# FFN down projections with one 512-column matmul per activation block for its high and low part

## The chip, the cores and the metric

The kernel runs on one core of one Trainium2 chip. The metric is device time in microseconds (us) of one launch. Durations of single instructions are in nanoseconds (ns).

## The reference

Two stacked transformer blocks of two layers each, on 256 tokens (T) of width 1024. There are eight SwiGLU feed-forward parts (FFNs); all else (attention of several kinds, retention, gated linear attention, cross attention, projections) is not touched by the change. An FFN is

```python
def swiglu(h, w_in, w_out):
    g, u = split_cols(h @ w_in, (D_FF, D_FF))      # D_FF = 2816
    return (jax.nn.silu(g) * u) @ w_out            # the last product is the "down projection"
x = x + 0.5 * swiglu(rms_norm(x, g), w_in, w_out)
```

Inputs and outputs are float32.

## The kernel before

Everything is kept transposed: a block is 128 channels (partitions) by 256 tokens. The 1024 channels are 8 blocks (KB), the 2816 hidden channels 22 blocks (HB). A product in nearly full precision is made of three matmuls in the float32r format: every weight tile `w` is split into `w_hi` (ScalarE, line 998) and `w_lo = w - w_hi` (VectorE, line 1410), every activation block into a high and a low part, and TensorE sums `w_hi*a_hi + w_hi*a_lo + w_lo*a_hi` in a PSUM bank.

The work of TensorE is a list of **units**. A unit is up to eight 128x128 weight tiles (k blocks) for one block of outputs, so 24 matmuls of 256 columns (18 where there are only six k blocks). Weights come from memory in loads of 1 MB (eight k blocks by 256 output channels, so two units) into a ring of four buffers, issued on SyncE's queue; the split weights lie in rings of four units. A splitting waits until the unit that used the slot four units earlier is done.

A **down projection** (`down0` to `down7`) has 8 output blocks. The 22 k blocks of an output are three units (8, 8 and 6 blocks); the two outputs of a 256-channel column chunk take turns, so their last units (two with 6 k blocks) come one after the other. That is 24 units and 528 matmuls for each down projection: 176 times `w_hi*hid_hi` (line 610), 176 times `w_hi*hid_lo` (line 611), and 176 times `w_lo*hid_hi` (line 614). Within a unit lines 610 and 611 alternate over the k blocks, and then line 614 runs over them. TensorE loads a weight tile before every matmul, also before the second that uses the same tile. The accumulator `acc` has four banks of 512 float32; a unit uses the first 256 columns of one (`out_ap`, line 491). Activations are in `hid_hi` and `hid_lo`, two tensors of 22 blocks.

The order of all work is written out by hand in one function `order`, which each engine goes through with its own stages. For a down projection the stage is `residual`. When an output block is complete, VectorE evicts it: line 1525 reads PSUM, scales it by 0.5 and by `rstd` (the norm's factor for each token) into `hidf`, waits for its own result (`link`), and line 1527 adds that to the residual stream `x`. Then it makes `w_lo` of a coming unit (`split_after`), and then the low part of the new `x` block for the next stage (`low`, line 1464), which waits for ScalarE's high part (line 1036). ScalarE squares the block (line 1040), and GpSimd adds the squares up (line 1924).

The next stage begins with a **leading pair** of units (`lead_pair`, lines 579 to 581): six matmuls for each block j, each j waiting for both parts of block j of the new `x`. Behind the pair TensorE takes the sum of the squares (line 649), for which it waits for GpSimd's last addition; where the next stage holds no values it then runs three small transposes of `x` (line 657) whose result nobody reads, and else two-column matmuls (line 652).

Of the kernel before, what the change touches and what calls it, by code (L numbers as in the profile page):

```python
# [9 lines left out]
F32R = mybir.dt.float32r  # L10
I32 = mybir.dt.int32
ALU = mybir.AluOpType
ACT = mybir.ActivationFunctionType
AX = mybir.AxisListType

P = 128
T = 256
# [3 lines left out]
HB = FF // P  # L21
# [7 lines left out]
BANKS = 4  # L29
# [153 lines left out]
def build(nc, io, out):  # L183
    loads, units, outs, lin = plan_stream(io)
# [3 lines left out]
    for _, kind in outs:  # L188
        count[kind] += 1
        freed.append((kind, count[kind]))  # L190
# [15 lines left out]
    with ExitStack() as ctx:  # L206
        def sb(name, shape, dt=F32):
            return ctx.enter_context(nc.sbuf_tensor(name, shape, dt))

        def sem(name):  # L210
            return ctx.enter_context(nc.semaphore(name))
# [9 lines left out]
        w_hi = sb("w_hi", [P, RING, 8, P], F32R)  # L221
        w_lo = sb("w_lo", [P, RING, 8, P], F32R)
# [9 lines left out]
        silu_g, hidf = gates_hid[:, 0:2, :], gates_hid[:, 2:4, :]  # L232
        small = sb("small", [P, 64])
        rstd = sb("rstd", [P, 2, T])
        wa2 = sb("wa2", [P, 512])
        pos = sb("pos", [P, T], I32)
        with nc.sbuf_tensor("hid_hi", [P, HB, T], F32R) as hid_hi, nc.sbuf_tensor("hid_lo", [P, HB, T], F32R) as hid_lo:
            pass

        work = sb("work", [P, 2 * HB, T])  # L240
        ident, ones, ones64, perm_rope, perm_ret = (mats[:, i, :] for i in range(5))
# [3 lines left out]
        acc = ctx.enter_context(nc.psum_tensor("acc", [P, BANKS, 512], F32))  # L245
# [5 lines left out]
        w_hi_ready, w_lo_ready, unit_done = sem("w_hi_ready"), sem("w_lo_ready"), sem("unit_done")  # L251
# [3 lines left out]
        silu_done, hid_mul, hid_hi_ready, hid_lo_ready = sem("silu_done"), sem("hid_mul"), sem("hid_hi_ready"), sem("hid_lo_ready")  # L255
# [235 lines left out]
        def out_ap(o):  # L491

            return acc[:, o % BANKS, 0:T]

        def wait_free(eng, o):

            if o >= BANKS:
                kind, n = freed[o - BANKS]
                eng.wait_ge((gate_evac, hid_mul, out_evac)[kind], n)
# [38 lines left out]
        fills = {"hn": (hn_hi, hn_lo, hn_hi_ready, hn_lo_ready), "mn": (mn_hi, mn_lo, mn_hi_ready, mn_lo_ready)}  # L538
# [25 lines left out]
        def _(pe):  # L564
            s = Stages()
            state = Progress()

            def lead_pair(i):
# [15 lines left out]
                if state.sums is not None:  # L584
                    sum_squares()

            def unit(i):
                u = units[i]
                if i in leaders:
                    return lead_pair(i)  # L590
                if i - 1 in leaders:
                    return
                if u.first:
                    wait_free(pe, u.out)
                pe.wait_ge(w_hi_ready, i + 1)
                if u.src == "hid":
                    a_hi, a_lo = hid_hi, hid_lo
                    pe.wait_ge(hid_hi_ready, u.need)
                    pe.wait_ge(hid_lo_ready, u.need)
                else:  # L600
                    a_hi, a_lo, r_hi, r_lo = fills[u.src]
                fresh = u.src != "hid" and (i == 0 or units[i - 1][8:10] + (units[i - 1].k0,) != u[8:10] + (u.k0,))
                if u.mode == "F":
                    wh, wl = w_hi[:, u.slot], w_lo[:, u.slot]
                    bank = out_ap(u.out)
                    for j in range(u.nk):
                        if fresh:
                            pe.wait_ge(r_hi, 8 * u.need + u.k0 + j + 1)
                            pe.wait_ge(r_lo, 8 * u.need + u.k0 + j + 1)
                        nc.tensor.matmul(bank, wh[:, j, :], a_hi[:, u.k0 + j, :], start=u.first and j == 0, stop=False)  # L610
                        nc.tensor.matmul(bank, wh[:, j, :], a_lo[:, u.k0 + j, :], start=False, stop=False)  # L611
                    pe.wait_ge(w_lo_ready, i + 1)
                    for j in range(u.nk):
                        mm = nc.tensor.matmul(bank, wl[:, j, :], a_hi[:, u.k0 + j, :], start=False,  # L614
                                              stop=u.last and j == u.nk - 1)
                else:

                    if fresh:
                        pe.wait_ge(r_hi, 8 * u.need + 8)
                        pe.wait_ge(r_lo, 8 * u.need + 8)  # L620
                    pair, t = u.slot - u.half, u.half
                    pe.wait_ge(w_hi_ready, i - u.half + 2)
                    pe.wait_ge(w_lo_ready, i - u.half + 2)
                    bank = out_ap(u.out).rearrange("p (s n) -> p s n", s=2)
                    for j in range(u.nk):
                        ah, al = a_hi[:, j, P * t:P * t + P], a_lo[:, j, P * t:P * t + P]
                        wh, wl = w_hi[:, pair:pair + 2, j, :], w_lo[:, pair:pair + 2, j, :]
                        nc.tensor.matmul(bank, ah, wh, start=j == 0, stop=False)  # L628
                        nc.tensor.matmul(bank, ah, wl, start=False, stop=False)  # L629
                        mm = nc.tensor.matmul(bank, al, wh, start=False, stop=j == u.nk - 1)  # L630
                mm.then_inc(unit_done, 1)

                if state.sums is not None and u.src == "hn" and i >= BANKS - 1:
                    sum_squares()
# [9 lines left out]
            def sum_squares():  # L644

                i, column = state.sums
                state.sums = None
                pe.wait_ge(squares_added, 7 * (i + 1))
                mm = nc.tensor.matmul(wide[:, 0, 0:T], ones, t1[:, 0, :], start=True, stop=True)
                if column:  # L650
                    for t in range(2):
                        mm = nc.tensor.matmul(wide[:, 1, 2 * t:2 * t + 2], t1[:, 0, P * t:P * t + P], ones[:, 0:2],
                                              start=True, stop=True)
                mm.then_inc(sums_done, 1)
                if not column:
                    for b in range(3):
                        nc.tensor.transpose(wide[:, 1, P * b:P * b + P], x[:, b, 0:P], ident)
# [735 lines left out]
        def _(dve):  # L1393
            s = Stages()
            state = Progress()

            def link(ins):

                state.chain += 1
                ins.then_inc(dve_chain, 1)  # L1400
                dve.wait_ge(dve_chain, state.chain)

            def split_after(i):

                while state.split < len(units) and (units[state.split].free or 0) <= i + 1:
                    n, u = state.split, units[state.split]
                    dve.wait_ge(w_hi_ready, n + 1)
                    if u.free is not None:
                        dve.wait_ge(unit_done, u.free)
                    nc.vector.tensor_tensor(w_lo[:, u.slot, 0:u.nk, :], raw[:, u.raw % RING, 0:u.nk, P * u.half:P * u.half + P],  # L1410
                                            w_hi[:, u.slot, 0:u.nk, :].bitcast(F32), ALU.subtract).then_inc(w_lo_ready, 1)
                    state.split = n + 1
# [102 lines left out]
            def residual(c, name, scale, gain):  # L1515
                l, later = lin[name], []
                if name in PARTED:
                    dve.wait_ge(out_evac, freed[l.o0 - 1][1])
                for n in range(l.u0, l.u1):
                    u = units[n]  # L1520
                    if u.last:
                        k = u.out - l.o0
                        dve.wait_ge(unit_done, n + 1)
                        if u.src == "hid":
                            link(nc.vector.scalar_tensor_tensor(hidf[:, k % 2, :], out_ap(u.out), scale, rstd[:, 0, :],
                                                                ALU.mult, ALU.mult))
                            nc.vector.tensor_tensor(x[:, k, :], x[:, k, :], hidf[:, k % 2, :], ALU.add).then_inc(out_evac, 1)
                        else:
                            nc.vector.tensor_tensor(x[:, k, :], x[:, k, :], out_ap(u.out), ALU.add).then_inc(out_evac, 1)
                        if gain is not None:  # L1530
                            later.append(k)
                    if n < l.u1 - (2 if name in PARTED else 1):
                        split_after(n)
                    for k in later:
                        low(k, c.gen, gain)
                    later = []
                split_after(l.u1 - 1)
                dve.wait_ge(out_evac, freed[l.o1 - 1][1])
# [543 lines left out]
```

## Time and profile before

| what | us |
|---|---|
| three runs shown | 2218.0, 2218.53, 2229.66; median 2218.53 |
| span of the profiled execution, first to last instruction | 2228.6 |
| its own time, taken to be the run of 2229.66 (the only one that is not shorter than the span) | 2229.66 |
| mean granted clock of TensorE in it | 0.994 of 2.4 GHz |
| TensorE busy with matmuls / weight loads | 2167.5 / 2123.3 |
| VectorE / ScalarE / GpSimd busy | 1508.9 / 1182.3 / 117.6 |

Matmuls overlap in the records, since the end of one is modelled with its way through the array. So what tells how fast TensorE works is the distance from one start to the next, or the number of matmuls in a stretch, and not a matmul's duration. Records are named by line, engine and operation, then output<-inputs (moving operand first, then the weights), shapes, and in brackets the idle time of the engine before it with what ended that.

### The profile page before, as it was taken

To read this page: it belongs to the slowest core of one execution; us is meant where nothing else is said; L and a number is where in the kernel's file an instruction comes from. 1 tells how busy PE (TensorE), PEld (TensorE's weight loads), DVE (VectorE), ACT (ScalarE), POOL (GpSimd) and SP (SyncE) were. 2 spreads that over 40 slices of the span, in tenths; PEclk is the share of its full clock that TensorE was granted. 3 is DMA by queue.
4 is the path that set the end of the run, shared out by engine and by line. 5 is a ranking of instruction groups with operands and counts; after the bars stand their busy time and mean duration, and the time that the engine had idled before them with its cause. 6 is when DMAs were issued, how large, how long until landed. Compare 5 with 4: busy or idle time off the path is not lost.

```text
span 2228.6 us, 44915 instructions
## 1 busy us (share of the span) xinstructions
PE 2167.5 (97%) x18339; PEld 2123.3 (95%) x18339; DVE 1508.9 (68%) x2244; ACT 1182.3 (53%) x1852; POOL 117.6 (5%) x140
## 2 busy tenths in 40 slices
PE   5999999999999999999999999999999999999998
PEld 5999987899999999989999999989999999999998
DVE  5756668676667666686766666688666666667664
ACT  5644455565456444465654554546655554556543
POOL 2101000110011000000100000100000000001001
PEclk9999999999999999999999999999999999999999
DMA  7556443365565656542765665644656665636653
GB/s 240 182 180 190 140 145 95 105 218 190 186 192 177 197 186 215 167 143 76 229 197 180 199 193 191 231 138 137 205 185 194 198 200 179 191 105 191 197 180 105
DMA packets 383402, 392.76 MB, mean 176 GB/s; under 512 B 6800, under 2 KB 381712, under 8 KB 383072
## 3 DMA queue, kind: packets, MB, share of 16 engines
q1 hardware_dynamic: 381632, 383.30, 53.8%
q0 software_dynamic: 1568, 6.59, 0.8%
q8 instruction: 148, 2.42, 0.5%
q14 instruction: 54, 0.44, 0.1%
HBM read 388.81 MB, written 1.05 MB: 175 GB/s over the span
## 4 chain that ended last, share of the span: by engine, by line
PE 86%; DVE 6%; ACT 4%; issue 2%; POOL 1%; DMA 1%; SPq 0%; POOLq 0%; ACTq 0%; DVEq 0%
PE acc L610 24%; PE acc L611 24%; PE acc L614 24%; DVE w_lo L1410 2%; PE acc L628 2%; PE acc L630 2%; PE acc L629 2%; ACT w_hi L998 2%; PE acc L579 1%; PE acc L581 1%; PE acc L580 1%; POOL t L1924 1%; DMA raw<-in_ffn_w_in 1%; PE wide L804 1%; PE wide L702 0%
## 5 line engine op out<-in xcount | busy, mean ns | idle before, releaser
L1410 DVE TENSOR_TENSOR w_lo<-raw,w_hi 128x1024 fp32r<-128x1024 f32 (+2 forms) x790 | 898.7, 1141 | 489.7 <-ACT w_hi L998 487.5
L998 ACT ACTIVATE w_hi<-raw 128x1024 fp32r<-128x1024 f32 (+2 forms) x790 | 775.6, 988 | 832.7 <-PE acc L614 755.2
L610 PE MATMUL acc<-hn_hi,w_hi 128*128 128x256 f32 x3328 | 791.9, 280 | 24.9 <-DMA colc<-in_cols 17.8
L611 PE MATMUL acc<-hn_lo,w_hi 128*128 128x256 f32 x3328 | 786.4, 278 | 0.0
L610 PEld LDWEIGHTS acc<-hn_hi,w_hi 128*128 128x128 f32 x3328 | 629.2, 189 | 29.0 <-DMA colc<-in_cols 17.8
L611 PEld LDWEIGHTS acc<-hn_lo,w_hi 128*128 128x128 f32 x3328 | 629.3, 189 | 0.6 <-issue 0.5
L614 PE MATMUL acc<-hn_hi,w_lo 128*128 128x256 f32 x3328 | 449.7, 278 | 0.0
L614 PEld LDWEIGHTS acc<-hn_hi,w_lo 128*128 128x128 f32 x3328 | 412.9, 189 | 0.0
L610 PE MATMUL acc<-hid_hi,w_hi 128*128 128x256 f32 x1408 | 331.6, 277 | 0.0
L611 PE MATMUL acc<-hid_lo,w_hi 128*128 128x256 f32 x1408 | 331.6, 277 | 0.0
L611 PEld LDWEIGHTS acc<-hid_lo,w_hi 128*128 128x128 f32 x1408 | 264.8, 188 | 0.0
L610 PEld LDWEIGHTS acc<-hid_hi,w_hi 128*128 128x128 f32 x1408 | 264.8, 188 | 0.0
L1924 POOL TENSOR_TENSOR t<-t 128x256 f32<-128x256 f32 x119 | 107.2, 901 | 2102.0 <-ACT t L1040 2054.7
L614 PE MATMUL acc<-hid_hi,w_lo 128*128 128x256 f32 x1408 | 192.4, 277 | 0.0
L614 PEld LDWEIGHTS acc<-hid_hi,w_lo 128*128 128x128 f32 x1408 | 175.2, 188 | 0.0
L610 PE MATMUL acc<-mn_hi,w_hi 128*128 128x256 f32 x512 | 131.6, 293 | 4.5 <-DVE mn_lo L1512 3.7
L611 PE MATMUL acc<-mn_lo,w_hi 128*128 128x256 f32 x512 | 125.8, 282 | 0.0
L610 PEld LDWEIGHTS acc<-mn_hi,w_hi 128*128 128x128 f32 x512 | 98.1, 192 | 7.0 <-issue 6.7
L1545 DVE TENSOR_TENSOR gates_hid<-acc,rstd 128x256 f32<-128x256 f32 x176 | 74.4, 423 | 37.8 <-PE acc L614 26.8
L611 PEld LDWEIGHTS acc<-mn_lo,w_hi 128*128 128x128 f32 x512 | 98.0, 191 | 1.4 <-issue 1.2
L1554 DVE TENSOR_TENSOR gates_hid<-gates_hid,acc 128x256 f32<-128x256 f32 x176 | 73.9, 420 | 28.6 <-PE acc L614 26.9
L1464 DVE SCALAR_TENSOR_TENSOR hn_lo<-x,gains,hn_hi 128x256 fp32r<-128x256 f32 x112 | 79.2, 712 | 12.3 <-ACT hn_hi L1036 12.3
(250 smaller groups left out, 2178.1 us busy)
## 6 DMA issues: line engine op xcount, KB each, us to landing
raw<-in_ffn_w_in SPq DMA_DIRECT2D x88, 1024.0 KB, 5.2
raw<-in_ffn_w_out SPq DMA_DIRECT2D x32, 1024.0 KB, 5.3
raw<-in_ffn_pre_w_gate SPq DMA_DIRECT2D x22, 1024.0 KB, 5.4
raw<-in_ffn_pre_w_up SPq DMA_DIRECT2D x22, 1024.0 KB, 5.4
raw<-in_ffn_post_w_gate SPq DMA_DIRECT2D x22, 1024.0 KB, 5.3
raw<-in_ffn_post_w_up SPq DMA_DIRECT2D x22, 1024.0 KB, 5.4
raw<-in_x_w_kv SPq DMA_DIRECT2D x16, 1024.0 KB, 5.5
raw<-in_ffn_pre_w_down SPq DMA_DIRECT2D x16, 1024.0 KB, 5.1
```

What stands on the lines that cost most here:

```text
L610: nc.tensor.matmul(bank, wh[:, j, :], a_hi[:, u.k0 + j, :], start=u.first and j == 0, stop=False)
L611: nc.tensor.matmul(bank, wh[:, j, :], a_lo[:, u.k0 + j, :], start=False, stop=False)
L614: mm = nc.tensor.matmul(bank, wl[:, j, :], a_hi[:, u.k0 + j, :], start=False, stop=u.last and j == u.nk - 1)
L628: nc.tensor.matmul(bank, ah, wh, start=j == 0, stop=False)
L629: nc.tensor.matmul(bank, ah, wl, start=False, stop=False)
L630: mm = nc.tensor.matmul(bank, al, wh, start=False, stop=j == u.nk - 1)
L998: nc.scalar.activation(w_hi[:, u.slot, 0:u.nk, :], raw[:, u.raw % RING, 0:u.nk, P * u.half:P * u.half + P], ACT.Copy).then_inc(w_hi_ready, 1)
L1410: nc.vector.tensor_tensor(w_lo[:, u.slot, 0:u.nk, :], raw[:, u.raw % RING, 0:u.nk, P * u.half:P * u.half + P], w_hi[:, u.slot, 0:u.nk, :]. ...
L1464: nc.vector.scalar_tensor_tensor(hn_lo[:, k, :], x[:, k, :], gains[:, gain + k:gain + k + 1], hn_hi[:, k, :].bitcast(F32), ALU.mult, ALU.s ...
L1545: nc.vector.tensor_tensor(silu_g[:, h, :], out_ap(units[u0 + h].out), rstd[:, 0, :], ALU.mult)\
L1554: nc.vector.tensor_tensor(hidf[:, h, :], silu_g[:, h, :], out_ap(units[u0 + 2 + h].out), ALU.mult).then_inc(hid_mul, 1)
L1924: nc.gpsimd.tensor_tensor(t1[:, 0, :], t1[:, 0, :], t1[:, k, :], ALU.add).then_inc(squares_added, 1)
```

## The change

High and low part of a hidden block lie side by side in one tensor, and one matmul with 512 columns takes both into the two halves of the bank. The part with `w_lo` is added to the first half as before. The eviction first adds the two halves with a `tensor_reduce` over a strided view of the bank, and the scaling then reads its result from SBUF instead of PSUM.

```diff
-        with nc.sbuf_tensor("hid_hi", [P, HB, T], F32R) as hid_hi, nc.sbuf_tensor("hid_lo", [P, HB, T], F32R) as hid_lo:
-            pass
+        with nc.sbuf_tensor("hid", [P, HB, 2, T], F32R) as hid:
+            hid_hi, hid_lo = hid[:, :, 0, :], hid[:, :, 1, :]
...
+        def both_out(o):
+
+            return acc[:, o % BANKS, 0:2 * T]
...
+            def hidden_unit(i):
+
+                u = units[i]
+                if u.first:
+                    wait_free(pe, u.out)
+                pe.wait_ge(w_hi_ready, i + 1)
+                pe.wait_ge(hid_hi_ready, u.need)
+                pe.wait_ge(hid_lo_ready, u.need)
+                for j in range(u.nk):
+                    nc.tensor.matmul(both_out(u.out), w_hi[:, u.slot, j, :], hid[:, u.k0 + j, :, :].rearrange("p s t -> p (s t)"),
+                                     start=u.first and j == 0, stop=False)
+                pe.wait_ge(w_lo_ready, i + 1)
+                for j in range(u.nk):
+                    mm = nc.tensor.matmul(out_ap(u.out), w_lo[:, u.slot, j, :], hid[:, u.k0 + j, 0, :], start=False,
+                                          stop=u.last and j == u.nk - 1)
+                mm.then_inc(unit_done, 1)
...
                         if u.src == "hid":
-                            link(nc.vector.scalar_tensor_tensor(hidf[:, k % 2, :], out_ap(u.out), scale, rstd[:, 0, :],
+                            link(nc.vector.tensor_reduce(hidf[:, k % 2, :], both_out(u.out).rearrange("p (s t) -> p t s", s=2),
+                                                         AX.X, ALU.add))
+                            link(nc.vector.scalar_tensor_tensor(hidf[:, k % 2, :], hidf[:, k % 2, :], scale, rstd[:, 0, :],
                                                                 ALU.mult, ALU.mult))
                             nc.vector.tensor_tensor(x[:, k, :], x[:, k, :], hidf[:, k % 2, :], ALU.add).then_inc(out_evac, 1)
```

`unit` calls `hidden_unit` for the units of the down projections; their waits are the same as before. All other units are unchanged.

## Rows read from the trace of the kernel before

**Rows 1.** The page's first part: busy us, share, instructions.

```profile
PE 2167.5 (97%) x18339; PEld 2123.3 (95%) x18339; DVE 1508.9 (68%) x2244; ACT 1182.3 (53%) x1852; POOL 117.6 (5%) x140
```

**Rows 2.** The page's costliest groups: matmuls of the down projections; last, idle before.

```profile
L610 PE MATMUL acc<-hid_hi,w_hi 128*128 128x256 f32 x1408 | 331.6, 277 | 0.0
L611 PE MATMUL acc<-hid_lo,w_hi 128*128 128x256 f32 x1408 | 331.6, 277 | 0.0
...
L614 PE MATMUL acc<-hid_hi,w_lo 128*128 128x256 f32 x1408 | 192.4, 277 | 0.0
```

**Rows 3.** Stretches: us, busy (count) of PE, PEld, DVE, ACT, POOL; PEclk, DMA share, GB/s.

```profile
154.00:216.00 62.00, 62.00 (x529) 62.00 (x528) 37.18 (x46) 29.61 (x39) 4.38 (x5) 1.00 0.60 189
597.00:656.00 59.00, 59.00 (x523) 59.00 (x523) 36.53 (x47) 28.82 (x38) 4.25 (x5) 1.00 0.60 192
783.00:844.00 61.00, 61.00 (x520) 61.00 (x520) 36.25 (x46) 28.68 (x38) 4.41 (x5) 1.00 0.57 182
```

**Rows 4.** Timeline of PE, start and us: line 614 of successive units, down0 and down1.

```profile
155.75 1.10 PE L614 MATMUL acc<-hid_hi,w_lo 128*128 128x256 f32 x8
158.57 1.10 PE L614 MATMUL acc<-hid_hi,w_lo 128*128 128x256 f32 x8
...
601.36 1.07 PE L614 MATMUL acc<-hid_hi,w_lo 128*128 128x256 f32 x8
604.08 1.07 PE L614 MATMUL acc<-hid_hi,w_lo 128*128 128x256 f32 x8
```

**Rows 5.** Timeline of PE's weight loads before matmuls 256, 2 and 512 wide.

```profile
427.80 1.27 PEld L773 LDWEIGHTS wide<-work 128*128 128x128 f32 x6
429.10 1.08 PEld L783 LDWEIGHTS wide<-mats,t 128*128 128x128 f32 x8
430.09 0.19 PEld L610 LDWEIGHTS acc<-hn_hi,w_hi 128*128 128x128 f32 x1
...
924.81 0.19 PEld L686 LDWEIGHTS wide<-t,mats 128*128 128x128 f32 x1 [0.24 <-issue]
...
926.96 0.19 PEld L686 LDWEIGHTS wide<-t,mats 128*128 128x128 f32 x1 [0.24 <-issue]
```

**Rows 6.** Busy time by stretch, columns as in rows 3: up parts, and behind down2.

```profile
100.00:150.00 50.00, 50.00 (x427) 50.00 (x426) 31.81 (x45) 24.59 (x36) 0.00 (x0) 1.00 0.59 191
...
664.00:688.00 24.00, 24.00 (x214) 24.00 (x213) 17.74 (x25) 17.38 (x30) 5.75 (x6) 1.00 0.64 211
...
720.00:770.00 50.00, 50.00 (x427) 50.00 (x426) 34.46 (x50) 26.50 (x40) 0.00 (x0) 1.00 0.66 212
860.00:910.00 50.00, 50.00 (x427) 50.00 (x426) 38.39 (x59) 18.90 (x18) 0.00 (x0) 1.00 0.62 197
...
1280.00:1330.00 50.00, 50.00 (x443) 50.00 (x443) 33.71 (x48) 24.77 (x37) 0.00 (x0) 1.00 0.61 190
```

**Rows 7.** Groups of DVE by line and shape: busy us, mean ns.

```profile
L1527 DVE TENSOR_TENSOR x<-x,gates_hid 128x256 f32<-128x256 f32 x64 | 27.4, 428 | 2.2
L1525 DVE SCALAR_TENSOR_TENSOR gates_hid<-acc,rstd 128x256 f32<-128x256 f32 x64 | 26.6, 415 | 6.7 <-PE acc L614 6.7
...
L1626 DVE TENSOR_REDUCE small<-prob 128x2 f32<-128x512 f32 x16 | 10.8, 676 | 0.0
...
L1582 DVE SCALAR_TENSOR_TENSOR t<-keep,gains,t 128x256 f32<-128x256 f32 x16 | 7.5, 479 | 4.5 <-ACT t L1028 4.5
```

**Rows 8.** Timeline of DVE, then POOL and PE, where down1 ends at 656.6.

```profile
655.54 0.43 DVE L1527 TENSOR_TENSOR x<-x,gates_hid 128x256 f32<-128x256 f32 x1
655.99 1.23 DVE L1410 TENSOR_TENSOR w_lo<-raw,w_hi 128x1024 fp32r<-128x1024 f32 x1
657.13 0.97 DVE L1464 SCALAR_TENSOR_TENSOR hn_lo<-x,gains,hn_hi 128x256 fp32r<-128x256 f32 x1
658.02 0.41 DVE L1525 SCALAR_TENSOR_TENSOR gates_hid<-acc,rstd 128x256 f32<-128x256 f32 x1
...
659.46 0.48 DVE L1464 SCALAR_TENSOR_TENSOR hn_lo<-x,gains,hn_hi 128x256 fp32r<-128x256 f32 x1 [0.58 <-ACT hn_hi L1036]
...
659.82 0.73 POOL L1924 TENSOR_TENSOR t<-t 128x256 f32<-128x256 f32 x1 [2.00 <-ACT t L1040]
...
661.43 0.28 PE L579 MATMUL acc<-hn_hi,w_hi 128*128 128x256 f32 x1
...
662.11 0.59 PE L649 MATMUL wide<-t,mats 128*128 128x256 f32 x2
```

**Rows 9.** Timeline at the end of down7, the last projection of the kernel.

```profile
2218.83 0.42 DVE L1525 SCALAR_TENSOR_TENSOR gates_hid<-acc,rstd 128x256 f32<-128x256 f32 x1 [1.16 <-PE acc L614]
...
2221.01 0.70 PE L649 MATMUL wide<-t,mats 128*128 128x256 f32 x2 [2.22 <-POOL t L1924]
```

More of the change, by code:

```diff
@@ L592, in unit @@
                     return
+                if u.src == "hid":
+                    return hidden_unit(i)
                 if u.first:
@@ L595, in unit @@
                 pe.wait_ge(w_hi_ready, i + 1)
[L596 to L602, printed above, removed]
+                a_hi, a_lo, r_hi, r_lo = fills[u.src]
+                fresh = i == 0 or units[i - 1][8:10] + (units[i - 1].k0,) != u[8:10] + (u.k0,)
                 if u.mode == "F":
```

## The prediction

> **What bounds the kernel now.** I read the page's busy shares first: TensorE's matmuls cover 97% of the span, its weight loads 95%, VectorE 68% [rows 1]. Then the groups of the down projections: 3 x 1408 matmuls, and no idle time of TensorE before any of them [rows 2]. So the down projections are bound by TensorE, and what one matmul costs there is the distance between two starts. The busy time by stretch gives it by count: down1 runs 523 matmuls in 59.0 us, 112.8 ns each, and down0 529 in 62.0 us, 117.2 ns [rows 3]. The timeline gives it exactly: a unit of 24 matmuls takes 604.08 - 601.36 = 2.72 us in down1, 113.3 ns for each, and 158.57 - 155.75 = 2.82 us in down0, 117.6 ns [rows 4]. So there are **two paces**, at the same granted clock (1.00, which is 2.4 GHz) in both [rows 3]. Down0 and down2 went at the slow pace, the other six at the fast one (their stretches count 523 matmuls in 59 us, as down1). The pace holds for long stretches and is not bound to the code: the up part of the third FFN began fast behind down1 (214 in 24 us), then turned slow and stayed so through down2 and behind it (427 in 50 us); the first FFN was slow too, the up part of the fifth fast (443) [rows 6]. That is much of what separates the runs: the 11 us between this execution's own time (2229.66, its span of 2228.6 and about 1.1 around it) and the median of 2218.53 are 2500 slow matmuls at 4.4 ns, more than either slow stretch holds (some 200 us, 1700 to 1850 matmuls). So the median run had at most one of the two slow down projections.
>
> **The merged pair, the main term.** 1408 pairs of 256-column matmuls with the same weights become 1408 matmuls of 512 columns. A pair costs 2 x 113.3 = 226.7 ns, or 235.2 at the slow pace. What will 512 columns cost? That depends on what the 113.3 are: the streaming of the columns, or the weight load before each. The load's own pace shows where matmuls have only 2 columns: from the first to the last of the group starting at 429.10, to 430.09, is 0.99 us for 8 loads, of which the first distance is still that of the 256-wide one before it (the group at 427.80 has (429.10 - 427.80)/6 = 217 ns each); the other seven take (990 - 217)/7 = 110 ns [rows 5]. So a weight load alone takes 110 ns, nearly the whole 113.3. The streaming: plain float32 matmuls with 512 columns start (926.96 - 924.81)/5 = 430 ns apart, those with 256 columns 217 [rows 5], so 256 more columns cost 213 and the fixed part is about 3 ns. Float32 takes over 1.9 times as long for a column as float32r (430/512 against 113.3/256), so I take it to stream everything twice: 512 float32r columns then stream as 256 float32 ones, in **216 ns**, with the load of the next tile hidden under them (the load takes 110 of the 216 there too). The bounds: below, 213 (the columns alone); above, 226.7 (nothing gained). I take 216, the row with as much streaming and one load. Saved: 10.8 ns a pair at the fast pace, 19.3 at the slow one; 1408 x 10.8 = 15.2 us, and for each slow down projection another 176 x 8.5 = 1.5.
>
> The Trainium skill, "TensorE: Matmul & The Clock Gate", section "Back-to-back issue gap", gives N/2.4 + 2.5 ns for a lone matmul: 109.2 ns for 256 columns and 215.8 for 512. The trace agrees for the wide float32 ones and not for the 256-wide float32r ones, which take 113.3. By that rule a merger would save one fixed part, 2.5 ns, and the whole change 3.5 us before its costs; it is the second rival below.
>
> **The remaining narrow matmuls.** The 1408 with `w_lo` keep 256 columns, in runs of 8 or 6 behind 512-wide ones. Which pace a run takes is drawn anew after each break in the stream, and no row shows it behind 512-wide float32r matmuls. All fast costs nothing; all slow costs 1408 x 4.4 = 6.2 us against a fast execution. With no reason for either I take the middle, 3.1 us (and half of it, 0.4 us, back for each down projection that was slow).
>
> **The eviction, 64 times.** It gains a reduction over 512 elements: 676 ns by the reduction with 512 inputs [rows 7]. Bounds: below, 0.42 (a 256-wide instruction), above 1.23, the row with 1024 elements [rows 8], if each short sum of two costs double. Line 1525 goes from reading PSUM (415 ns) to two operands in SBUF, 479 as line 1582 [rows 7], and the extra link costs about 0.04. Together 0.78 us. In the middle of a down projection this is hidden: VectorE is busy 36.5 of 59 us [rows 3], and 8 x 0.78 = 6.2 us more still leaves 16 us idle; `w_lo` is made for a unit that runs three units, some 8 us, later. Memory has room too (0.60 busy in these stretches). The changed layout of `hid` changes no instruction's size.
>
> **Where the cover is thin: the end of a down projection, 7 times.** VectorE is late there already. Last matmul of down1 at 656.6; its eviction starts only at 658.02, behind the eviction of block 6, a `w_lo` and a `hn_lo`; `hn_lo` of block 7 ends at 659.94, and the leading pair needs it at 661.43: 1.49 us of slack. The sum of squares needs GpSimd's 660.55 at 662.11: 1.56 [rows 8]. Both evictions grow: 2 x 0.78 = 1.56 us; and TensorE arrives about 0.13 earlier (two short units, each 6 x 10.8 ns less). 1.69 against 1.49 minus about 0.05 for the signal: it waits some 0.25 us, 7 x 0.25 = 1.8 us. **At the very end** nothing covers it: from line 1525 at 2218.83 to TensorE's sum at 2221.01 each step waits for the last [rows 9], so 0.8 us more.
>
> **The sum.** On the profiled execution: 15.2 + 2 x 1.5 for the pairs, -3.1 + 2 x 0.4 for the narrow ones, -1.8, -0.8: 13.3 us, 2229.66 to 2216.4. On the median run, with none or one slow down projection: 9.5 to 11.4. I take 11: **2207.5 us**. That is 0.50%, just where a measurement of this kernel can tell it from no change.
>
> **Rivals.**
> 1. *The 113.3 ns are streaming and a fixed part, and the load was hidden anyway.* The fixed part would be 113.3 - 106.5 = 6.8 ns (half of the 213 for 256 columns), and a merger saves just that: 9.6 us, and no narrow matmul changes pace. With the exposed 2.6: 7 us, 2211.5. For it: a slow pace that adds a fixed 4.4 ns. Against it: the load pace of 110, and 3 ns of fixed part in the float32 rows [rows 5]. 0.12.
> 2. *Only the 2.5 to 3 ns of fixed part are saved* (the skill's rule above, and by rows 2 x 217 - 430 = 4 ns): 1408 x 3 = 4.2, minus 2.6: 2217. Against it: 256 columns would have to come at 109, and never do. 0.04.
> 3. *The eviction costs what its upper bound says* (1.23 instead of 0.68): each of two evictions is 0.55 later, 1.1 us more waiting at 7 ends and 0.55 at the last, 8.3 us in all: 2215.8. 0.08.
> 4. *The other side: the narrow matmuls fall into the slow pace and carry it on.* The pace outlives the end of a down projection (down2 slow, and behind it 427 in 50 us [rows 3, 6]). If the short runs always end slow: 6.2 us for the `w_lo` ones, and, where they were fast, the three up parts that directly follow down1, down3 and down5 (1056 matmuls each, 14 us) plus the first projections behind down4 and down6 (some 440, 2 us): 22 us lost against 15.2 - 2.6 gained, so 2228. It decides from 12.6 us/4.4 ns = 2860 matmuls made slow. Against it: behind down1 and down3 the pace was fast [rows 6]. 0.07.
> 5. *512-wide float32r streams at float32's rate* (430 ns): 1408 x 203 ns = 286 us, 2504. Nothing speaks for it but that no row shows the shape. 0.01.
>
> The skill also has a rule for the other direction (same page, Part 3, section "The mechanism"): a weight load overlaps a running matmul only in other row groups. Every removed load would then save its full length, by our row 110 ns, 155 us in all. But two starts 113.3 apart leave no room for 106 of columns and 110 of load in series, so I give it no chance of its own.
>
> The forecast has 0.68.
>
> **The chances.** Within the forecast the gain is 12.6 (all narrow ones fast) to 6.4 (all slow), more with slow down projections to win back: somewhat more than half of it beyond 11.1 us, 0.41; the rest 0.27. Rivals 1 to 3 mostly lie within 0.5%, 0.03 of them faster and 0.01 (the eviction) slower. Rival 4's 2228 is 0.43% above the median: half of it counts as slower, and rival 5 does. Faster 0.44, same 0.50, slower 0.06. The range reaches from both slow down projections won back with everything fast (2218.5 - 15.2 - 3.0 = 2200) over rivals 1 to 3 to a little beyond no change, 2220.
>
> **What would show it.** Starts of 512-wide matmuls 216 ns apart (rival 1: 220; 2: 224; nothing gained: 226.7), so a full unit in 2.63 us, and a down projection in 57.9 instead of 59.8 us; the `w_lo` matmuls at 113 or 118. Reductions of 0.68 us on 64 evictions. At the seven ends a wait of 0.1 to 0.4 us of the leading pair for `hn_lo`, where there is none now. A TensorE that waits inside a down projection, for `w_lo`, `w_hi` or a bank, would prove the cover argument wrong; up parts that begin at 427 in 50 us behind down1, down3 and down5 would be rival 4.

## The result and the profile after

| | median us | range, runs | ratio to before (95% interval) |
|---|---|---|---|
| before | 2222.63 | 2218.0 to 2229.66, 5 | |
| changed | 2235.29 | 2231.42 to 2236.06, 5 | 1.0051 (1.0030 to 1.0072) |
| changed again, on another chip | 2230.67 | 2225.78 to 2236.69, 12 | 1.0035 (1.0021 to 1.0048) |

The ratio of the third line is to `before` on that chip, 2223.94 us. The change makes the kernel slower by 0.35 to 0.5%. Forecast were 2207.5 us and a range of 2200 to 2220, counted from 2218.53, the median of the three runs of `before` that had been shown; over five runs it is 2222.63. The profiled execution has a span of 2231.1 us.

The group lines of the changed kernel's page show what became of [rows 2]:

```profile
L600 PE MATMUL acc<-hid,w_hi 128*128 128x512 f32 x1408 | 358.7, 395 | 0.0
L600 PEld LDWEIGHTS acc<-hid,w_hi 128*128 128x128 f32 x1408 | 250.3, 188 | 45.4
...
L604 PE MATMUL acc<-hid,w_lo 128*128 128x256 f32 x1408 | 191.8, 277 | 0.0
```

Half of the loads for `w_hi` are gone, and the loads now have idle time (45.4 us) that the matmuls do not have (0.0): the next weights are there early, as forecast, and TensorE is still never idle. So the question is how far apart the starts are. The timeline of PE in down1 (start, us):

```profile
593.71 2.02 PE L600 MATMUL acc<-hid,w_hi 128*128 128x512 f32 x8
595.57 1.07 PE L604 MATMUL acc<-hid,w_lo 128*128 128x256 f32 x8
596.48 2.02 PE L600 MATMUL acc<-hid,w_hi 128*128 128x512 f32 x8
598.34 1.07 PE L604 MATMUL acc<-hid,w_lo 128*128 128x256 f32 x8
```

Eight wide matmuls take 595.57 - 593.71 = 1.86 us, **232.5 ns each** (232.65 over all starts of down1), where two narrow ones took 226.7 and 216 was forecast. The distances are not even: the first wide matmul of a unit, behind a narrow one, takes 226 ns as two narrow ones do, and the others 235, 231, 236, 231 and so on. Eight narrow ones take 0.91 us, 114 ns. A unit takes 2.77 us instead of 2.72 (or 2.82 at the slow pace) [rows 4]. Every down projection now takes 60.9 us from first to last start, whatever the pace before it: six were 59.7 before, and down0 and down2 62.1.

VectorE and TensorE where down1 ends (its last matmul starts at 654.61), to be set beside [rows 8]:

```profile
656.60 0.68 DVE L1543 TENSOR_REDUCE gates_hid<-acc 128x256 f32<-128x512 f32 x1
657.31 0.43 DVE L1545 SCALAR_TENSOR_TENSOR gates_hid<-gates_hid,rstd 128x256 f32<-128x256 f32 x1
657.77 0.43 DVE L1547 TENSOR_TENSOR x<-x,gates_hid 128x256 f32<-128x256 f32 x1
658.77 0.48 DVE L1482 SCALAR_TENSOR_TENSOR hn_lo<-x,gains,hn_hi 128x256 fp32r<-128x256 f32 x1 [0.58 <-ACT hn_hi L1054]
...
659.48 0.28 PE L583 MATMUL acc<-hn_hi,w_hi 128*128 128x256 f32 x1
```

The reduction takes 0.68 us; the low part of block 7 ends at 659.25 and is needed at 659.48. The slack shrank from 1.49 to 0.23 us, and no wait came of it. At the end of the kernel, where [rows 9] had 2.22 us of idle time before the sum:

```profile
2223.26 0.98 PE L667 MATMUL wide<-t,mats 128*128 128x256 f32 x2 [2.95 <-POOL t L1944]
```

2.95 - 2.22 = 0.73 us more is exposed.

### The profile page after: what moved, and what is told of

It reads as the page before. It is cut to its first block, busy times and chain, and to the rows that moved or that the text cites. A ratio compares the mean times of both kernels' runs of the same rounds, so it can differ in the third digit from the quotient of the medians.

```text
span 2231.1 us, 42163 instructions
## 1 busy us (share of the span) xinstructions
PE 2170.3 (97%) x16931; PEld 2062.4 (92%) x16931; DVE 1549.7 (69%) x2308; ACT 1178.1 (53%) x1852; POOL 114.5 (5%) x140
## 3 DMA queue, kind: packets, MB, share of 16 engines
HBM read 388.81 MB, written 1.05 MB: 175 GB/s over the span
## 4 chain that ended last, share of the span: by engine, by line
PE 86%; DVE 6%; ACT 4%; issue 2%; POOL 1%; DMA 1%; SPq 0%; POOLq 0%; ACTq 0%; DVEq 0%
PE acc L628 17%; PE acc L629 17%; PE acc L632 17%; PE acc L600 15%; PE acc L604 7%; DVE w_lo L1428 2%; PE acc L646 2%; ACT w_hi L1016 2%; PE acc L648 2%; PE acc L647 2%; PE acc L583 1%; PE acc L585 1%; PE acc L584 1%; POOL t L1944 1%; DMA raw<-in_ffn_w_in 1%
## 5 line engine op out<-in xcount | busy, mean ns | idle before, releaser
L600 PE MATMUL acc<-hid,w_hi 128*128 128x512 f32 x1408 | 358.7, 395 | 0.0
L600 PEld LDWEIGHTS acc<-hid,w_hi 128*128 128x128 f32 x1408 | 250.3, 188 | 45.4
L604 PEld LDWEIGHTS acc<-hid,w_lo 128*128 128x128 f32 x1408 | 189.3, 188 | 17.4
L604 PE MATMUL acc<-hid,w_lo 128*128 128x256 f32 x1408 | 191.8, 277 | 0.0
L1054 ACT ACTIVATE hn_hi<-x,gains 128x256 fp32r<-128x256 f32 x112 | 56.1, 507 | 94.9 <-DVE x L1547 73.3
L632 PE MATMUL acc<-mn_hi,w_lo 128*128 128x256 f32 x512 | 78.5, 281 | 0.0
```

The lines of the kernel that those rows point to most:

```text
L600: nc.tensor.matmul(both_out(u.out), w_hi[:, u.slot, j, :], hid[:, u.k0 + j, :, :].rearrange("p s t -> p (s t)"), start=u.first and j == 0, ...
L604: mm = nc.tensor.matmul(out_ap(u.out), w_lo[:, u.slot, j, :], hid[:, u.k0 + j, 0, :], start=False, stop=u.last and j == u.nk - 1)
L1054: nc.scalar.activation(hn_hi[:, k, :], x[:, k, :], ACT.Copy, scale=gains[:, gain + k:gain + k + 1])\
```

## The experiments

Lengths of down projections below are from the first to the last start of their matmuls. "Before" is measured anew with each set, on the same chip.

### The parts of the change, each alone

`e1_halves`: the new eviction with narrow matmuls.

```diff
-                    nc.tensor.matmul(both_out(u.out), w_hi[:, u.slot, j, :], hid[:, u.k0 + j, :, :].rearrange("p s t -> p (s t)"),
-                                     start=u.first and j == 0, stop=False)
+                    for s in range(2):
+                        nc.tensor.matmul(both_out(u.out)[:, T * s:T * s + T], w_hi[:, u.slot, j, :], hid[:, u.k0 + j, s, :],
+                                         start=u.first and j == 0 and s == 0, stop=False)
```

> Keeps the new layout and the new eviction, but goes back to two 256-column matmuls, high part into the first half of the bank, low part into the second. Theory 'matmul' (the whole loss is the 512-wide matmuls' 232.65 ns where two narrow ones take 226.7): down projections take 59.7 us again at the fast pace (62.1 at the slow), the eviction costs only its exposed part at the very end, 0.8 to 1.0 us, so about 2224 against 2222.6 before. Rival 'eviction' (the later x blocks delay the next stages): the time stays near the changed kernel's, 2233 to 2235, with waits of the leading pairs.

`e2_wide_old_evict`: the wide matmuls with the eviction of before.

```diff
-                            link(nc.vector.tensor_reduce(hidf[:, k % 2, :], both_out(u.out).rearrange("p (s t) -> p t s", s=2),
-                                                         AX.X, ALU.add))
-                            link(nc.vector.scalar_tensor_tensor(hidf[:, k % 2, :], hidf[:, k % 2, :], scale, rstd[:, 0, :],
+                            link(nc.vector.scalar_tensor_tensor(hidf[:, k % 2, :], out_ap(u.out), scale, rstd[:, 0, :],
```

> The 512-wide matmuls with the old eviction, which reads the first half alone (the product with the low activation part is computed but left out of the result). Theory 'matmul': every down projection takes 60.9 us as in the changed kernel, the time is 1 us below the changed kernel's, 2232 to 2234. Rival 'eviction': near the kernel before, 2223.

Measured: `e1_halves` 2226.87 us beside 2227.78 of before, ratio 0.9997 (0.9983 to 1.0011); `e2_wide_old_evict` 2230.14, ratio 1.0014 (1.0003 to 1.0025). The new eviction alone costs nothing that can be measured in the whole; the wide matmuls alone make the kernel slower. The two parts add up to 0.11%, less than the 0.35 and 0.51% of the whole change; the intervals reach 0.11 to 0.14% to either side for the parts and up to 0.21% for the whole, so the sizes of the parts are not settled by these ratios. The lengths of the down projections are sharper. Unit starts in `e1_halves` are 2.72 us apart in down1, in `e2_wide_old_evict` 2.78:

```profile
597.21 1.07 PE L605 MATMUL acc<-hid,w_lo 128*128 128x256 f32 x8
599.93 1.07 PE L605 MATMUL acc<-hid,w_lo 128*128 128x256 f32 x8
```

```profile
596.77 1.07 PE L604 MATMUL acc<-hid,w_lo 128*128 128x256 f32 x8
599.55 1.07 PE L604 MATMUL acc<-hid,w_lo 128*128 128x256 f32 x8
```

In the profile of `e1_halves` six down projections took 59.7 us, and down0 and down2 62.1, as in that of before; in `e2_wide_old_evict` all took 60.9. At the ends of the five fast down projections of `e1_halves` that a leading pair follows, the distance before the matmul that needs block 7 is 0.19 us in place of 0.11, a wait of 0.08 us; the changed kernel has none. The absolute times missed (2224 and 2232 to 2234 were expected). Before itself was 5 us longer on this chip than in the first five runs, which covers the first miss. It makes the second one larger: `e2_wide_old_evict` came out 2.4 us above before, and some 10 were expected. Its profile has the 60.9 us that were expected in every down projection; before on this chip has no profile, so how many of its down projections were slow is not known.

### Does the weight load set the pace?

`e3_before_m64`: the kernel before, but the down projections use 64 of the 128 columns of each weight tile, so half of their outputs are left out. `e4_after_m64`: the same in the changed kernel, for wide and narrow matmuls, with the old eviction (the product with the low activation part is left out too). Both, like all runs below for which no ratio is given, were executed once and serve for their distances, not for their times.

```diff
+                    if u.src == "hid":
+                        wh, wl, bank = wh[:, :, 0:64], wl[:, :, 0:64], bank[0:64]
```

```diff
-                    nc.tensor.matmul(both_out(u.out), w_hi[:, u.slot, j, :], hid[:, u.k0 + j, :, :].rearrange("p s t -> p (s t)"),
+                    nc.tensor.matmul(both_out(u.out)[0:64], w_hi[:, u.slot, j, 0:64], hid[:, u.k0 + j, :, :].rearrange("p s t -> p (s t)"),
...
```

> Kernel before, but the down projections use 64 of the 128 columns of each weight tile (half of the outputs left out), so each weight load is half as long. Theory 'stream' (113.3 ns is what 256 float32r columns take to stream; the load is hidden): starts stay 113.3 or 117.8 ns apart, a down projection 59.7 or 62.1 us. Rival 'load' (my prediction's: the load sets the 113.3): 109 ns apart, 57.5 us a down projection.

> 512-wide matmuls with 64 of the 128 weight columns and the old eviction (half of the outputs, and the low activation part, left out). Theory 'stream': 226 to 236 ns for a wide matmul as in the changed kernel, 60.9 us a down projection, perhaps down to 226.7 ns each (59.8 us) if the load under the stream is what adds the last 6 ns. Rival 'load' (a load under a stream takes a share of it that goes with its length): 216 to 224 ns, below two narrow ones.

The record of a load gets shorter with the columns, from 188 to 134 ns (the second number from the end). `before`, then `e3_before_m64`:

```profile
L610 PEld LDWEIGHTS acc<-hid_hi,w_hi 128*128 128x128 f32 x1408 | 264.8, 188 | 0.0
```

```profile
L612 PEld LDWEIGHTS acc<-hid_hi,w_hi 128*64 128x64 f32 x1408 | 188.9, 134 | 0.0
```

Timeline of PE in `e3_before_m64`, down0 and down1:

```profile
157.93 1.12 PE L616 MATMUL acc<-hid_hi,w_lo 128*64 128x256 f32 x8
160.79 1.11 PE L616 MATMUL acc<-hid_hi,w_lo 128*64 128x256 f32 x8
...
601.93 1.07 PE L616 MATMUL acc<-hid_hi,w_lo 128*64 128x256 f32 x8
604.65 1.07 PE L616 MATMUL acc<-hid_hi,w_lo 128*64 128x256 f32 x8
```

A unit in down1 takes 2.72 us, 113.3 ns a matmul, **to the digit as with full tiles**; the slow pace went from 117.8 to 119.1 (2.86 us). In `e4_after_m64`:

```profile
593.68 2.02 PE L600 MATMUL acc<-hid,w_hi 128*64 128x512 f32 x8
595.54 1.11 PE L604 MATMUL acc<-hid,w_lo 128*64 128x256 f32 x8
```

the wide matmuls are still 232.5 ns apart (the narrow ones behind them 118 in place of 114, which makes a down projection 61.5 us; why a shorter load makes them slower is not known, as with the 119.1). Half the columns of the load change neither 113.3 nor 232, and the changed kernel, which has half as many loads for `w_hi`, gains nothing by it: the theory "load" on which my main term stood falls.

### What of the stream is slow?

`e5_w384`: 384 columns instead of 512 (the low part of the last 128 tokens is left out), old eviction. `e10_two_places`: the whole changed kernel, high and low part 22 KB apart. `e6_bf16` and `e9_bf16_dense`: both operands of the wide matmul read as bfloat16, once with the columns four bytes apart (the upper halves of the float32 elements), once two bytes apart; the eviction is the old one. The first of these computes the product with `w_hi` coarsely and leaves out the low activation part; the second reads 512 halves of elements that lie side by side, which is another product, and its eviction multiplies by 0.

```diff
+                    nc.tensor.matmul(both_out(u.out)[:, 0:384], w_hi[:, u.slot, j, :], hid[:, u.k0 + j, :, :].rearrange("p s t -> p (s t)")[:, 0:384],
```

```diff
+        with nc.sbuf_tensor("hid", [P, 2, HB, T], F32R) as hid:
+            hid_hi, hid_lo = hid[:, 0, :, :], hid[:, 1, :, :]
...
+                    nc.tensor.matmul(both_out(u.out).rearrange("p (s t) -> p s t", s=2), w_hi[:, u.slot, j, :], hid[:, :, u.k0 + j, :],
...
```

```diff
+                    nc.tensor.matmul(both_out(u.out), w_hi[:, u.slot, j, :].bitcast(BF16)[:, 1:2 * P:2],
+                                     hid[:, u.k0 + j, :, :].rearrange("p s t -> p (s t)").bitcast(BF16)[:, 1:4 * T:2],
...
+                                     hid[:, u.k0 + j, :, :].rearrange("p s t -> p (s t)").bitcast(BF16)[:, 0:2 * T],
```

> The matmul with w_hi takes 384 columns instead of 512 (the low activation part of the last 128 tokens left out), with the old eviction. Theory 'stream' (float32r columns come at 113.3/256 = 0.443 ns each or slower, whatever the width): 170 to 176 ns. Rival 'fixed' (columns come at 213/512 = 0.417 ns, and what is above that is a fixed part of a matmul, 19 ns for the wide one): 160 + 19 = 179 ns.

> 512-wide matmul with both operands read as bfloat16 (the upper two bytes of each float32 element, so in steps of four bytes), the w_lo one unchanged in float32r, with the old eviction. Theory 'bytes' (the array is fed four bytes a column and that read is what takes 0.443 ns or more): 216 ns a wide matmul, the 213 of its columns and the 3 of a fixed part. Rival 'place' (the distance of the columns in memory, the bank's write or something outside TensorE slows it): 226 to 236 as before.

> As the bfloat16 run, but the 512 columns lie next to each other (two bytes apart, so half as many bytes are passed over). Result of the product with w_hi and low/high parts meaningless, so the eviction scales it by 0. Theory 'bytes passed over' (the read of the moving operand, by the memory it passes over, sets 0.44 ns a column): 216 ns a wide matmul against 226 with the four-byte steps. Rival 'width' (something that goes by columns, such as the write to the bank): 226 again.

> The changed kernel, but high and low part in two separate halves of the tensor (22 KB apart in each partition) instead of side by side; one matmul still takes both. If it matters that the 512 columns are one run of memory, the distance changes from 232.65 ns (226.7 would be two narrow ones); if the stream is slow by its width alone, 232.65 and 60.9 us a down projection again.

`e5_w384` and `e10_two_places`, PE:

```profile
587.19 1.54 PE L600 MATMUL acc<-hid,w_hi 128*128 128x384 f32 x8
588.58 1.07 PE L604 MATMUL acc<-hid,w_lo 128*128 128x256 f32 x8
```

```profile
595.85 2.02 PE L600 MATMUL acc<-hid,w_hi 128*128 128x512 f32 x8
597.71 1.07 PE L604 MATMUL acc<-hid,w_lo 128*128 128x256 f32 x8
```

384 columns take (588.58 - 587.19)/8 = 174 ns (172.9 over all starts), so a fixed 19 ns is out (179 expected). The place in memory does not matter: 1.86 us for eight, 60.9 us a down projection, the same as the changed kernel.

The bfloat16 runs, by the weight loads, whose starts follow those of the matmuls; first the four-byte steps, then the dense ones:

```profile
591.92 1.23 PEld L601 LDWEIGHTS acc<-hid,w_hi 128*128 128x128 bf16 x6
593.28 1.11 PEld L606 LDWEIGHTS acc<-hid,w_lo 128*128 128x128 f32 x8
```

```profile
593.11 0.96 PEld L601 LDWEIGHTS acc<-hid,w_hi 128*128 128x128 bf16 x5
594.19 0.19 PEld L606 LDWEIGHTS acc<-hid,w_lo 128*128 128x128 f32 x1
```

(593.28 - 591.92)/6 = **227 ns** with four-byte steps, (594.19 - 593.11)/5 = **216 ns** with two-byte steps; over all down projections, behind another wide one, 226.8 and 216.3. The bank is written alike in both, with 512 float32 columns, and the weights are the same. Only the read of the moving operand differs: its step, with that the memory that it passes over, and its values. So the 216 ns of my forecast exist, but for an operand of two bytes a column; at four bytes a column the stream is slower, and float32r is slower still (232.65). The rival "width" is out, since a bank takes 512 columns in 216 ns. "Bytes" in the form that I gave it before `e6_bf16` (216 for the element type alone) was wrong too. Whether it is the bytes passed over that cost the 11 ns, or the step of two elements, is not shown, and neither is what costs float32r the last 6. A down projection takes 60.1 us in `e6_bf16` and 58.7 in `e9_bf16_dense`, where the narrow matmuls behind the wide ones take 116.4 ns on average, so not even 216 ns for the wide ones gave the 57.9 of the forecast.

The Trainium skill, "SBUF — State Buffer", section "A bandwidth-pool intuition that's wrong (but worth ruling out)", gives TensorE's moving operand 2 bytes per lane and cycle at 2.4 GHz. Read as a limit, it would make 512 float32r columns take 427 ns, an estimate from that figure; the runs have 232.65. The same page, section "Door 1: The DMA port swizzle (why `[64,N]` ≈ `[32,N]`)", says that each access which crosses to a new 16-byte line pays a penalty, but also that two accesses to a line are enough for full speed. Dense bfloat16 columns make eight accesses to a line and four-byte steps four, so by the first half the dense run should be faster and by the second both the same. Measured are 216 and 227; and it says nothing of the step from 227 to 232.65, where the columns lie alike.

### Can the order within a unit mend it?

`e7_interleaved`: each narrow matmul right behind the wide one of its block.

```diff
+                pe.wait_ge(w_lo_ready, i + 1)
                 for j in range(u.nk):
                     nc.tensor.matmul(both_out(u.out), w_hi[:, u.slot, j, :], hid[:, u.k0 + j, :, :].rearrange("p s t -> p (s t)"),
                                      start=u.first and j == 0, stop=False)
-                pe.wait_ge(w_lo_ready, i + 1)
-                for j in range(u.nk):
                     mm = nc.tensor.matmul(out_ap(u.out), w_lo[:, u.slot, j, :], hid[:, u.k0 + j, 0, :], start=False,
```

> Changed kernel with each narrow w_lo matmul right behind the wide one of the same block, instead of eight wide and then eight narrow. In the changed kernel the wide one behind a narrow one took 226 and the narrow one behind a wide one 118. Theory 'stream' with an extra that only follows a wide one: 226.7 + 118 = 344.5 ns a block, a down projection 60.6 us. Rival: the extra goes with the wide one wherever it stands, 232.65 + 114 = 346.7, 61.0 us. Time in both cases that of the changed kernel within 3 us.

Both theories missed. Time 2245.07, ratio 1.0095 (1.0077 to 1.0114), and a down projection takes 62.1 us:

```profile
597.32 0.40 PE L601 MATMUL acc<-hid,w_hi 128*128 128x512 f32 x1
597.55 0.28 PE L603 MATMUL acc<-hid,w_lo 128*128 128x256 f32 x1
597.67 0.40 PE L601 MATMUL acc<-hid,w_hi 128*128 128x512 f32 x1
```

A block takes 0.35 us, 235 for the wide one and 118 for the narrow, without a wait. That is the slow pace for everything: 235 is twice 117.8. The eight down projections account for 9.3 of the 14 us above the changed kernel on the same chip; where the rest lies is open. Reading the changed kernel's first wide matmul (226 behind a narrow one) as a rule for all was wrong.

### The changed kernel once more, and the pace of the rest held alike

`e8_changed` is the changed kernel on another chip.

> The changed kernel again, beside the others on one chip. From the down projections' lengths (60.9 against 59.7 us fast, 62.1 slow) and the exposed 1 us it should be 0 to 10 us above the kernel before, by how many of the down projections of before run at the slow pace; middle 0.2 to 0.4%.

Measured: the third line of the first table, 1.0035, at the middle of what was expected. Its down1 shows 329 matmuls in 57 us, as in the first profile.

`e11_reset` is the kernel **before** with three transposes more at each of eight places, of three kinds; `e12_changed_reset` is the changed kernel with the same.

```diff
                 mm.then_inc(sums_done, 1)
-                if not column:
-                    for b in range(3):
-                        nc.tensor.transpose(wide[:, 1, P * b:P * b + P], x[:, b, 0:P], ident)
+                settle(2 if column else 1)
+
+            def settle(bank):
+                for b in range(3):
+                    nc.tensor.transpose(wide[:, bank, P * b:P * b + P], x[:, b, 0:P], ident)
...
                         nc.tensor.matmul(wide[:, 1, 0:T], ones, t1[:, 0, :], start=True, stop=True).then_inc(sums_done, 1)
+                        settle(2)
+                    if n is not None and j == 20:
+                        settle(2)
```

> Kernel before, plus three small transposes at each place from which a slow stretch began: behind the sums of squares that had none, and in the first and third FFN behind the sum for the memory norm and behind the unit that waits for a bank. In the trace of before the pace was fast behind every one of the seven places that have them. Theory 'the pace is set by what precedes': up0, down0, up2 and down2 all fast, down projections all 59.7 us, 5 to 12 us below before (0.2 to 0.5%), with a narrower spread of the runs. Rival 'chance': some of these stretches are slow again, and the time is before's plus 2 us for the transposes.

> The changed kernel with the same added transposes. With the pace of all else held fast, the difference to the run with transposes alone is the change itself: 8 x (60.9 - 59.7) = 9.4 us and 1 us for the last eviction, 10 us or 0.47%. Rival: the difference is under 5 us, then the change's loss lay in the pace of other stages.

Measured, side by side on one chip: before 2223.46 (21 runs, 2215.7 to 2230.49); `e11_reset` **2218.94** (10 runs, 2215.33 to 2221.93), ratio 0.9972 (0.9958 to 0.9987); `e12_changed_reset` 2228.82 (12 runs, 2226.71 to 2232.22), ratio 1.0019 (1.0005 to 1.0034). The two differ by 9.9 us, where 10 was expected. The runs of `e11_reset` lie in two groups (2215.3 to 2217.7, and 2220.2 to 2221.9) with the median between them, so this difference is good to some 3 us. With that, the change itself costs about 10 us when the rest goes at nearly one pace. The smaller ratios of the plain comparisons fit down projections that were slow in before. One more thing adds to that: both profiles of the changed kernel ran the up part ahead of down0 fast (444 and 443 matmuls from 100 to 150 us) where that of before ran it slow, 552 matmuls or 2.4 us. Whether the change brings that about is not shown; `e2_wide_old_evict`, which has the wide matmuls too, has 427 there.

Stretches of `e11_reset` (us, busy and count of PE first), to be set beside the 427 in 50 us of [rows 6]:

```profile
64.00:82.00 18.00, 18.00 (x156) 18.00 (x155) 10.72 (x20) 10.84 (x17) 0.00 (x0) 1.00 0.53 177
100.00:150.00 50.00, 50.00 (x444) 50.00 (x443) 32.66 (x46) 25.62 (x38) 0.00 (x0) 1.00 0.58 188
...
720.00:770.00 50.00, 50.00 (x444) 50.00 (x443) 33.39 (x47) 24.72 (x37) 0.00 (x0) 1.00 0.61 197
```

The long stretches went fast (444 in 50 us), and all eight down projections took 59.7 us. But 64 to 82 us, right behind the first added transposes, was slow (156 in 18 us; `e12_changed_reset` has 161 there), and so was the same place of the third FFN, 684 to 702 us (155). So the transposes do not fix the pace everywhere, and the theory holds in part only. The gain of 4.5 us is just under the 5 to 12 that were expected. The spread of the runs did narrow, from 14.8 to 6.6 us, though over fewer runs. The fastest run of before, 2215.7, is as short as that of `e11_reset`: the long runs are gone, no shorter ones came. By the median `e11_reset` is the fastest version with the full computation.

## Why the prediction was wrong

**What bounds the kernel** held: TensorE has no idle time in the down projections, before and after. Two paces exist. That they are what separates runs of one kernel is argued from one trace of it, and fits the narrower spread of `e11_reset`; no two traces of before show it.

**The step that failed is "I take 216, the row with as much streaming and one load".** It had two legs. One was the weight load: its own pace of 110 ns lay so near 113.3 that I read it as the cause. `e3_before_m64` halves the columns of the load and 113.3 stays. The other was the price of streaming, taken from float32 rows by the guess that they stream everything twice. The rows did not carry it. They have a factor of 1.90 for a record, not 2, and a record is half a matmul: the one matmul of line 649 stands as x2 in [rows 8], and its two records start 216 ns apart. So 256 float32 columns take some 430 ns, 3.8 times what float32r takes. The guess gave 0.417 ns a column, a rate that float32r never reaches here: 113.3 for 256, 172.9 for 384, 232.65 for 512. Measured in place of 10.8 ns saved for each pair: 6.0 ns lost, or 1.05 us in each down projection. The upper bound, 226.7 as "nothing gained", was no bound. It supposed that a merger cannot be worse than its parts. By the three widths, each 128 columns beyond the first 256 cost 59.6 and 59.8 ns, and the first 256 cost 113.3, less than twice that. The forecast had the term as a gain of 15.2 us plus 1.5 for each slow down projection. Measured with the narrow matmuls of the next paragraph, it was a loss of 1.17 us in each of the six down projections that had been fast in the profile of before, and a gain of 1.17 in down0 and down2.

**Rivals 1 and 2** asked only how much of a fixed part is saved, and both put the wide matmul under 226.7; rival 1's 220 is as wrong as the forecast's 216. **Rival 5** had the right direction and place, a stream slower by its shape, with a price from a row far off and a chance of 0.01. The slower side should have had a moderate price there: a wide matmul a few ns above two narrow ones.

**The narrow matmuls.** I took the middle of two paces drawn by chance, 3.1 us. In each down projection they took 114.0 ns, hardly above the fast pace: 0.1 us each, 1 us in all. The draw was not by chance but the same in each unit.

**The eviction** was sized rightly: 0.68 us by the row of a reduction with the same input count, and rival 3 (1.23) is out. It grew by 0.73 us where I had 0.78. In the middle it was hidden: the down projections of `e1_halves` take the same 59.7 and 62.1 us as those of before.

**The thin cover.** I had 0.25 us of waiting at each of seven ends: 1.56 us of later evictions and TensorE 0.13 earlier. Counted from the start of the last matmul of a fast down projection, the low part of block 7 ends after 3.39 us in before and after 4.74 in `e1_halves`, so the evictions cost 1.35, and there a wait of 0.08 us came. In the changed kernel it is 4.65, since the wide matmuls of the last two units take longer, not less, than the narrow ones; the slack is 0.23 us, and no wait came. **The very end** cost 0.73 us more idle time before the sum, forecast 0.8.

**Rival 4** did not come true: in the changed kernel's trace the next stage went on fast behind down1, down3 and down5.

**The rule for a lone matmul.** The Trainium skill, "TensorE: Matmul & The Clock Gate", section "Back-to-back issue gap", puts it 2.5 ns above the columns, 215.8 ns for 512. That fits the dense bfloat16 run, 216, and no float32r matmul: for 256, 384 and 512 columns it gives 109.2, 162.5 and 215.8, and measured are 113.3, 172.9 and 232.65.

## What to carry to other kernels

Fewer and wider matmuls saved nothing here, where the weight load did not set the distance between starts. That a load takes nearly as long as that distance is no proof that it sets it; a run with half the weight columns tells. Price a wider instruction from rows of the same element type, look how many records one instruction leaves before you read a price off a record, and don't take "nothing gained" for the worst case. Where stretches of a kernel can go at another pace, count matmuls in fixed stretches of each trace first, or a gain of some us will be read out of the noise.

## What the runs showed of the hardware

- A 512-column matmul, starts apart: 216 ns with bfloat16 columns two bytes apart, 227 with bfloat16 columns four bytes apart, 232.65 with float32r, all at a granted clock of 1.00. 384 float32r columns 172.9, 256 in a steady stream 113.3 or 117.8.
- Halving the weight columns left the fast narrow pace (113.3) and the wide one (232) unchanged, and made the slow narrow pace (117.8 to 119.1) and the narrow matmuls behind wide ones (114 to 118) slower.
- The one float32 matmul of line 649, 256 columns wide, leaves two records that start 216 ns apart.
- With three transposes that nobody reads at each of eight places more, the kernel was 0.28% faster (ratio 0.9958 to 0.9987), and the long stretches of its trace went at the fast pace. What sets the pace, and why the wide float32r matmul costs more than two narrow ones, stays open.
